# A thirteenth slot for gathered rows, and half the scratch for dynamic transfers

## The reference, cut to what matters

```python
def peer_ffn(h, w_q, sub_keys, u_tab, v_tab):
    ...
    experts = i1 * PEER_KEYS + i2
    gates = jax.nn.softmax(best_s, axis=-1)
    ...
    def chunk(args):
        hh, ee, gg = args
        u_sel = u_tab[ee].astype(jnp.float32)
        v_sel = v_tab[ee].astype(jnp.float32)
        act = jax.nn.gelu(jnp.einsum('td,tkd->tk', hh, u_sel))
        return jnp.einsum('tk,tkd->td', gg * act, v_sel)

def reference(x, ...):
    for l in range(DEPTH):
        x = mixer_sublayer(x, ...)
        x = x + peer_ffn(rms_norm(x, norm2_g[l]), peer_wq[l], peer_keys[l], peer_u[l], peer_v[l])
    return x
```

## Time and profile before

| | |
|---|---|
| median of 3 runs | 1639.59 us (1638.54 to 1640.44) |
| profiled execution, its own time | 1639.44 us |
| its span in the trace | 1637.6 us |
| DVE busy | 1116.6 us, 68% |
| PE busy | 1079.0 us, 66% |
| POOL busy | 665.4 us, 41% |
| ACT busy | 431.1 us, 26% |
| DMA, mean over the span | 381 GB/s |
| first gather issued | 145.2 us |
| last gather issued | 1607.5 us |

### The profile page before, as it was taken

The page is one execution under the profiler, slowest core; times in us unless marked ns, Lnnn a source line. Parts: engine busy times, 40 slices in busy tenths (PEclk is TensorE's granted clock), DMA queues, the critical chain, the costliest instruction groups (busy, mean ns, idle before and its releaser), DMA issues. The chain is left out here.

```text
span 1637.6 us, 19577 instructions
## 1 busy us (share of the span) xinstructions
PE 1079.0 (66%) x6936; PEld 560.8 (34%) x6936; DVE 1116.6 (68%) x2614; ACT 431.1 (26%) x1118; POOL 665.4 (41%) x793
## 2 busy tenths in 40 slices
PE   7795665777576576676677586667766656555654
PEld 6665331442343143332254243434244311111111
DVE  3833999755599957666379968656469975455455
ACT  2221332341233320234033331225133321111111
POOL 6002333685285344334433353344333354444431
PEclk9998786988788688888888797888878876787688
DMA  9005999979999899999999999999999999999997
GB/s 392 22 30 224 419 419 358 420 308 399 397 419 390 353 419 419 420 419 420 420 382 420 419 412 420 419 419 419 420 392 419 414 372 420 420 419 420 419 419 319
DMA packets 86067, 623.52 MB, mean 381 GB/s; under 512 B 9809, under 2 KB 9809, under 8 KB 10961
## 3 DMA queue, kind: packets, MB, share of 16 engines
q0 software_dynamic: 73728, 536.90, 79.8%
q1 hardware_dynamic: 12240, 85.37, 12.8%
HBM read 621.19 MB, written 1.05 MB: 380 GB/s over the span
## 5 line engine op out<-in xcount | busy, mean ns | idle before, releaser
L455 POOL DMA_INDIRECT slot<-experts,idx x512 | 570.5, 1114 | 928.6 <-PE acc L1348 722.4
L1038 DVE CUSTOM_DVE_ANT_0 slot<-slot,h 128x1024 f32<-128x1024 f32 x512 | 616.4, 1230 | 348.8 <-DMA slot<-experts,idx 337.5
L1348 PE MATMUL acc<-slot,diag 64*64 64x512 f32 x4080 | 612.3, 751 | 366.3 <-ACT diag L732 365.6
L1348 PEld LDWEIGHTS acc<-slot,diag 64*64 64x64 f32 x4080 | 179.2, 168 | 745.4 <-ACT diag L732 442.0
L732 ACT ACTIVATE diag<-cst,ge 128x64 f32<-128x64 f32 x510 | 136.2, 336 | 149.1 <-DVE ge L758 133.8
L723 ACT ACTIVATE ge<-ge 128x4 f32<-128x4 f32 x129 | 26.5, 206 | 475.5 <-DVE ge L1038 474.6
L1315 PE MATMUL PB<-hT,ring 128*128 128x128 f32 x1024 | 129.8, 289 | 14.1 <-DMA ring<-weights 9.8
L1315 PEld LDWEIGHTS PB<-hT,ring 128*128 128x128 f32 x1024 | 126.2, 205 | 16.7 <-issue 10.9
L723 ACT ACT_TABLE_LOAD x56 | 71.8, 1283 | 28.4 <-DVE ge L1038 27.5
L716 ACT ACTIVATE rs<-bs 128x1 f32<-128x1 f32 x32 | 6.5, 203 | 235.0 <-DVE bs L973 227.6
L1288 PE MATMUL PX<-ring,work 128*128 128x512 f32 x96 | 51.5, 686 | 16.7 <-DVE work L948 16.7
(11 more groups left out here) (227 smaller groups left out, 1143.7 us busy)
## 6 DMA issues: line engine op xcount, KB each, us to landing
ring<-weights SPq DMA_DIRECT2D x32, 1152.0 KB
ring<-weights SPq DMA_DIRECT2D x28, 1024.0 KB
slot<-weights SPq DMA_DIRECT2D x12, 1024.0 KB, 21.7
slot<-experts,idx POOLq DMA_INDIRECT x512
sml<-small SPq DMA_DIRECT2D x2, 1160.0 KB, 11.1
xs<-x SPq DMA_DIRECT2D x2, 512.0 KB, 7.8
out<-xs SPq DMA_DIRECT2D x4, 256.0 KB
cst<-consts SPq DMA_DIRECT2D x1, 564.5 KB, 4.7
```

What stands on the lines that cost most here:

```text
L455: pool.indirect_dma_start(out=slot[:, E % SLOTS, :], out_offset=None, in_=src, in_offset=bass.IndirectOffsetOnAxis(ap=idx[:, n % 2, e:e + ...
L1038: ins = dve.tensor_tensor_reduce(u, u, h2[:, n % 2, :], 1.0, 0.0, ALU.mult, ALU.add, d[:, i:i + 1])
L1348: ins = pe.matmul(acc[HALF * half:HALF * half + HALF, i, :], diag[rows, d % DIAGS, :], slot[rows, E % SLOTS, D + half * 512:D + half * 512 ...
```

## The change

`SLOTS` goes from 12 to 13, so `slot` grows by 8 KB in each partition, and with it comes one more semaphore for landings. The scratch for dynamic transfers goes from 16,384 to 8,192 bytes of each partition, which frees just that room. Gather E now uses slot E % 13 and waits for pick E - 13. Slot 12 never holds a chunk, so the first gather into it has no wait on `chunk_used`.

```diff
-SLOTS = 12
+SLOTS = 13
...
                     if E < SLOTS:
 
-                        pool.wait_ge(S["chunk_used"], max(uses(0, E), uses(1, E) if in_slot(1, E) else 0))
+                        if E < CH_ROUTE:
+                            pool.wait_ge(S["chunk_used"], max(uses(0, E), uses(1, E) if in_slot(1, E) else 0))
                         pool.wait_ge(S["qkT_ready"], 2)
...
-    nc = _bacc.Bacc("TRN2", target_bir_lowering=False, num_devices=1)
+    nc = _bacc.Bacc("TRN2", target_bir_lowering=False, num_devices=1, dynamic_dma_scratch_size=8192)
```

## The result

| | before | after |
|---|---|---|
| median | 1640.02 us of 5 runs (1638.54 to 1643.98) | 1629.66 us of 5 runs (1626.69 to 1632.50) |
| profiled execution | 1639.44 us | 1632.50 us |
| its span | 1637.6 us | 1630.2 us |
| DVE, PE, POOL busy | 1116.6, 1079.0, 665.4 us | 1116.1, 1070.3, 673.7 us |

The kernel got faster by 0.6%: the ratio is 0.9936, with an interval of 0.9919 to 0.9952, which is 8 to 13 us. 1628.4 us had been forecast.

A forecast was written before the change was run, and what follows sets the result against it. The DMA stream of expert gathers (2.50 us each, 420 GB/s) was taken as the bound, with gain only from its dips: 1.2 + 1.2 + 2.5 + 2.5 + 1.4 + 2.2 = 11.0 us, 1639.4 to 1628.4 us, range 1618 to 1638.

The forecast's parts named there:

- (c): Dips at 510 to 553 us: 5.4 us unused, DVE-bound, so one gather can be won, 2.5 us.
- (d): Dip at 831 us: 2.5 us unused, DVE then waits at 852.77, so 2.5 us won.
- (f): Dips at 1309 and 1321 us: at most one gather, the two hold 2.2 us, all won ahead of the DMA-bound last stage.
- the scratch at nothing: Smaller scratch costs 0; the rival that it runs out and drains the DMA, say 1650 us, had chance 0.09.
- (a): 341 to 373 us, POOL's tables for the next layer: the chain starts earlier; 1.2 us for the first five dips together.
- (e): Dip at 1208 us: 1.4 us unused, DVE then waits 3.58 us at 1229.76, so 1.4 us won.
- (b): Dip at 444 us, end of the first tile's mixer: closes and passes on to DVE, 1.2 us.
- cap of one gather for each DVE-bound stretch: Where DVE is nearly always busy, the DMA gets ahead by one gather at most, 2.5 us, since slots are then full.
- the tables reset what was won before: POOL's table work at 341 to 373 us resets earlier gains, so the dips at 254 and 276 count for nothing.
- Chunk loads: PE waiting for a chunk in a dip could lose 1.4 us; taken as 0, with 5 us allowed in the range.
- every dip pays: Rival: each dip gives the smaller of itself and 2.5 us, 21.8 in all, so 1617.6 us; chance 0.13.
- the slot only fills earlier: Rival: PE and DVE carry on late, the extra gather just lies landed longer; 0 to 3 us, say 1637.5; chance 0.16.

The follow-up runs named there:

- e3: The changed kernel (after) unchanged, run again for a second trace beside the same runs of before: 1628.11 us, ratio 0.9925.
- e4: The changed kernel (after, 13 slots) with the scratch for dynamic transfers cut to 2,048 bytes: 1630.54 us, ratio 0.9934.
- e1: The kernel before, twelve slots, with only the scratch cut to 8,192 bytes: 1640.27 us beside 1641.28, ratio 0.9995.
- e2: The changed kernel with its 13 buffers and small scratch, but each gather waits for the pick twelve before it, as before: 1640.88 us, ratio 0.9998.
- e6: After with 14 slots, a scratch of 2,048 bytes and rB laid into a dead part of another buffer: 1628.47 us, ratio 0.9934.
- e7: After (13 slots) with POOL's table work, four blocks in quads 15 to 18, cut into 16 pieces over quads 13 to 24: 1622.83 us, ratio 0.9904.
- e8: The kernel before (12 slots) with the table work spread over quads 13 to 24 as in e7: 1631.13 us, ratio 0.9947.
- e12: e9 with two forced pauses of the gathers, ahead of gathers 288 and 400: 1612.67 us beside 1639.35, ratio 0.9843.
- e9: The 14 slots of e6 with the table work spread over quads 14 to 24: 1611.87 us, ratio 0.9831 against before.
- e10: After (13 slots) with the table work spread over quads 14 to 24, one quad later than e7: 1615.00 us, ratio 0.9859 against before.
- e11: After (13 slots) with one forced pause of the gathers ahead of gather 288, in which all DMA engines run empty: 1629.71 us, ratio 0.9940.

## Why the prediction came out right

The forecast of 11.0 us stands beside 10.4 by the medians, 13.2 in e3 (1641.28 - 1628.11), and 9.4 by the table of steps. What was right is the mechanism (an earlier release shortens the dips of the DMA, and DVE then waits less), the terms (c), (d) and (f), and the scratch at nothing. That the sum came out so close is in part luck: (a) was not seen, (e) was nearly all given back, and (b) brought almost three times its term.

*What bounds the kernel, and what a dip can give.* Held. The last stage still runs at share 1.01 and 420 GB/s, which is 2.50 us for a gather, and the gain came from dips alone. The cap of one gather for each DVE-bound stretch held for (c): 5.4 us were unused between 510 and 553, and 2.1 were won; from the packets of the six traces the unused time between 501 and 559 fell from 7.7 us to 4.8 in the mean. (f) can't tell, since its two dips together hold less than one gather (2.2 us; 1.8 were won).

*(a), 1.2 us for the table work: not seen.* The first half of the reasoning was right: the tables started 1.15 us earlier, at 315.36 instead of 316.51 (counted from the first dot product 1.6 us earlier in the mean of the six traces). But the step took it that the chain behind would move along, and pick 80 was reached no earlier (+0.3 us, good to about 2). In the profiled execution the first block of tables took 15.2 us instead of 12.3:

```profile
315.36 0.12 POOL L473 MEMSET base<- 128x8 f32 x1
...
315.57 2.39 POOL L425 TENSOR_TENSOR base<-base,tabp 128x8 f32<-128x8 f32 x2
318.05 0.31 POOL L478 TENSOR_SCALAR base<-base 128x32 f32<-128x32 f32 x1
318.44 1.16 POOL L480 TENSOR_SCALAR base<-base 128x16 f32<-128x16 f32 x1
319.56 0.25 POOL L481 TENSOR_SCALAR base<-base 128x16 f32<-128x16 f32 x1
...
320.97 1.18 POOL L491 TENSOR_SCALAR base<-base 128x16 f32<-128x16 f32 x1
...
323.65 0.20 POOL L491 TENSOR_SCALAR base<-base 128x16 f32<-128x16 f32 x1
...
330.86 2.03 POOL L456 DMA_INDIRECT slot<-experts,idx  x1 [0.27 <-POOL base L492]
```

The same instruction takes 0.20 us at 323.65 and 1.18 at 320.97. DVE in order of time shows what differs:

```profile
318.31 1.23 DVE L1039 CUSTOM_DVE_ANT_0 slot<-slot,h 128x1024 f32<-128x1024 f32 x1 [0.40 <-DMA slot<-experts,idx]
...
320.81 1.28 DVE L1039 CUSTOM_DVE_ANT_0 slot<-slot,h 128x1024 f32<-128x1024 f32 x1 [1.27 <-DMA slot<-experts,idx]
```

Each long one lies on a dot product. Over the trace of before, of the small table instructions behind 150 us, the 74 that meet no dot product take 0.23 us in the mean and 0.31 at most, the 25 that meet one 0.72 and up to 1.26; in after it is 0.23 (0.31) and 0.70 (1.28). A chain of dependent small instructions on POOL thus grows by how many dot products happen to fall on it, and the profiled execution met more of them. This is scatter and no reason for the missing gain: in e3 and e4 the block took 12.3 and 12.2 us, as in before, e1 and e2, and they reached pick 80 no earlier either. The second block scatters as much, 6.5 us in e1 against 8.2 to 9.5 in the other five. Next to that a gain of 1.2 us can't be told from none with three traces of each kind. The Trainium skill's page "SBUF — State Buffer" (SBUF: two separate sides) has the rule: VectorE and GpSimd share a port pair under an exclusive lock, held for a whole instruction, also where a VectorE operation has two SBUF inputs and the GpSimd one reads SBUF. The dot product has two SBUF inputs, and by that rule the trace agrees: the excess, 1.18 - 0.20 = 0.98 us, is no more than one dot product, 1.23.

*The claim beside it, that the tables reset what was won before, so that the dips at 254 and 276 count for nothing.* Borne out: with thirteen slots 1.7 us less are unused in these two dips and 2.1 us more in the table work (the table under e6). What e7 and e8 asked besides, whether the tables also hide some of the slot's worth, stays open. What the step lacked was that this stretch was worth more than the slot. The rows were there, and the earlier trace rows, where POOL itself is late; the prediction used them only to say that the slot could not help.

*(b), 1.2 us at 444: mis-sized, 3.3.* The dip closed as foreseen (its share is now 1.01). The prediction priced the term by the unused time of the dip, 1.2, and not by the wait of DVE that ended with it, 2.55 in the earlier trace rows. That wait fell whole: over picks 100 to 103 DVE waits for gathers 2.5, 2.4 and 3.3 us in the three traces before and 0.3, 0.0 and 0.0 in those after, and this is where 2.3 of the 3.3 us are won. Of the rest 0.3 lie between picks 80 and 100 and 0.6 between 104 and 112. It is not late gain of the table work, since nothing had been gained by pick 100. Where the DMA found the time beyond 1.2 us is not shown.

*(d), 2.5 us at 831: right*, 2.6.

*(e), 1.4 us at 1208: failed.* The dip was not closed; it is 2.2 us deep in after and 3.2 in e3, against 1.4. Between picks 320 and 360 1.7 us were won, but 1.4 us had been given back just before, between 231 and 320, where 0 was predicted: 0.3 us together. There the spread of the DMA engines grows, and DVE still waits for its gather behind the dip, as in the earlier trace rows:

```profile
1224.73 1.28 DVE L1039 CUSTOM_DVE_ANT_0 slot<-slot,h 128x1024 f32<-128x1024 f32 x1 [3.30 <-DMA slot<-experts,idx]
```

The packets of the six traces say where the 1.4 us were. When the DMA has moved as many bytes as picks 0 to 320 need, it is 8.8 us earlier than before, but pick 320 itself has landed only 6.3 us earlier: its last report comes 4.8 us behind that point, where it was 2.3. At pick 360 the lag is down to 1.7 us (2.2 before), and the stream is 8.1 us ahead. So what pick 320 lost is the lag of its slowest engine, and what was "won" up to pick 360 is that lag given back, while the dip itself took 0.7 us more. Against a gain by mending this stands e12: with the drift taken out by pauses, e9 did not get faster.

*The signs that were named.* The thirteenth gather starts 2.28 us behind the twelfth and not 1.25, because the twelfth took 1.98 us on POOL. The dips at 444 and 831 went, the one at 1208 did not. The two in the table work are still there, and deeper. Gathers of several us or pauses at even distances did not show.

*The scratch, 0: right*, by e1 and e4. *Chunk loads, 0 with up to 5 us for the range: right*, nothing of that kind shows. *The other rivals:* that every dip pays (1617.6) fails on (c) and the tables, where less was won than was unused; that the slot only fills earlier (1637.5) fails on (c), (d) and (f), where DVE did wait less.

## What to carry to other kernels

When a kernel is bound by one stream, list the dips of that stream with their unused time, and ask for each who ended it; a deeper queue helped here only where the consumer was late in releasing, and where the producer's own other work stands ahead (POOL's tables here) the DMA lost again what more buffers had won before it; moving that work was worth more (13 us by e10 over after) than one more buffer (10) or two (10). The value of a slot is not the same for each. Releases come in bursts here, which is the likely reason, though no run took it alone: the burst is four, twelve slots are a whole number of bursts, the first slot under that cost 25 us and the first above brought 10. Before buying space, look at what reserves it: the scratch for dynamic transfers could be cut to an eighth at no cost that shows.

## What the runs showed of the hardware

*The sixteen DMA engines can drift apart in a full stream.* With 12 gathers of 1 MiB in flight the first and last of the engines finish a gather 2 to 5 us apart, with 13 up to 8.2 (e3, 8.6 in e4), with 14 up to 9.6 (e6; means over 100 us), and a pause takes it back to 2.9 (e11). The growth stands between about 800 and 1200 us only; why there is not shown. The time from issue to landing in the last stage grew from 18.9 us (e1, 12 slots) to 22.1 (13) and 24.6 (14), about one gather's 2.50 us for each slot. The Trainium skill's page "DMA: Bandwidth & Descriptors" (Why a DMA increments its semaphore by 16 and not by 1) says that the engines finish independently and that each posts its own mark; these records show by how much, and that it is not constant.

*Small instructions on POOL take longer beside DVE's dot products*: 0.23 us alone, 0.70 to 0.72 in the mean and up to 1.28 beside one. The gathers themselves grow too, from 0.97 us in the mean (163 of them that meet no dot product, in before) to 1.18 (345 that do).

*The scratch for dynamic transfers* cost nothing at 8,192 bytes with 12 and 13 gathers in flight (e1, after), nor at 2,048 with 13 (e4). With 14 no larger scratch was run beside it.
